# Rotary embedding of the latent attention: a permutation matmul replaced by VectorE products written across partitions

## The reference, cut to what matters

```python
def _rope(x, base):                      # x: (B, S, ..., 64)
    x1, x2 = x[..., :half], x[..., half:]            # half = 32
    return concatenate([x1 * cos - x2 * sin, x2 * cos + x1 * sin], axis=-1)

k_rope = _rope(c[..., KV_LORA:], ROPE_BASE_B)        # once
q_rope = _rope(q[..., QK_NOPE:], ROPE_BASE_B)        # for each head
sc = (einsum('bqhd,bkhd->bhqk', qn_i, k_nope)
      + einsum('bqhr,bkr->bhqk', qr_i, k_rope)) * scale
```

## Time and profile before

| | us |
|---|---|
| median of 3 runs | 906.93 |
| lowest and highest | 906.9, 907.16 |
| the profiled execution's own time | 907.63 |
| its span, first to last instruction | 906.3 |
| TensorE busy | 894.1 (99%) |
| VectorE busy | 592.0 (65%) |
| ScalarE busy | 496.4 (55%) |
| GpSimd busy | 78.2 (9%) |

### The profile page before, as it was taken

One profiled execution on the slowest core, in us unless ns is written; L12 is line 12 of the kernel. 1 busy time (PEld: TensorE's weight loads), 2 busy tenths in 40 slices (PEclk: granted clock), 3 DMA queues, 4 the chain that ended last, 5 costly groups with the idle time before them and its releaser, 6 DMA issues.

```text
span 906.3 us, 13424 instructions
## 1 busy us (share of the span) xinstructions
PE 894.1 (99%) x5649; PEld 798.4 (88%) x5649; DVE 592.0 (65%) x793; ACT 496.4 (55%) x629; POOL 78.2 (9%) x58
## 2 busy tenths in 40 slices
PE   8999999999999999999999999999999999999998
PEld 7798887888899999998887899999899888888887
DVE  5876566559866666666478788766657665566441
ACT  5554444435756666665327677877654355445330
POOL 0010100000001111111000000222200012211000
PEclk9999999999999999999999999999999999999999
DMA  9834554642554444354465544232345535545630
GB/s 348 317 131 182 186 208 166 206 151 99 204 193 141 144 142 142 142 185 182 165 245 174 198 147 180 97 138 93 105 175 187 192 136 184 180 152 212 252 110 24
DMA packets 24829, 154.39 MB, mean 170 GB/s; under 512 B 3136, under 2 KB 3520, under 8 KB 9024
## 3 DMA queue, kind: packets, MB, share of 16 engines
q1 hardware_dynamic: 22880, 148.97, 45.2%
q10 hardware_dynamic: 1728, 4.02, 1.5%
q0 software_dynamic: 160, 0.52, 0.1%
HBM read 152.46 MB, written 1.05 MB: 169 GB/s over the span
## 4 chain that ended last, share of the span: by engine, by line
PE 88%; ACT 5%; DVE 4%; issue 2%; DMA 1%; SPq 0%; ACTq 0%
PE ps L338 23%; PE ps L340 23%; PE ps L339 23%; PE ps L389 7%; PE ps L392 3%; ACT w_hi_ring L966 1%; ACT c_p L1368 1%; PE ps L612 1%; DMA w_raw<-in_a_w_in 1%; PE ps L637 1%; PE ps L617 1%; PE ps L411 1%; PE ps L518 1%; PE ps L806 1%; PE ps L627 1%
## 5 line engine op out<-in xcount | busy, mean ns | idle before, releaser
L1409 DVE TENSOR_TENSOR w_lo_ring<-w_raw,w_hi_ring 128x2048 fp32r<-128x2048 f32 x146 | 341.3, 2351 | 202.2 <-ACT w_hi_ring L966 201.9
L966 ACT ACTIVATE w_hi_ring<-w_raw 128x2048 fp32r<-128x2048 f32 x146 | 277.4, 1910 | 110.9 <-PE ps L340 104.8
L338 PE MATMUL ps<-xT_hi,w_hi_ring 128*128 128x256 f32 x520 | 149.4, 287 | 2.9 <-DVE w_lo_ring L1415 1.7
L340 PE MATMUL ps<-xT_hi,w_lo_ring 128*128 128x256 f32 x520 | 147.0, 283 | 0.0
L339 PE MATMUL ps<-xT_lo,w_hi_ring 128*128 128x256 f32 x520 | 147.0, 283 | 0.0
L338 PE MATMUL ps<-w_hi_ring,xT_hi 128*128 128x512 f32 (+1 forms) x272 | 107.4, 395 | 1.4 <-DVE xT_lo L1586 0.6
L340 PE MATMUL ps<-w_hi_ring,xT_lo 128*128 128x512 f32 (+1 forms) x272 | 104.5, 384 | 0.0
L338 PEld LDWEIGHTS ps<-xT_hi,w_hi_ring 128*128 128x128 f32 x520 | 99.6, 192 | 5.5 <-issue 3.3
L339 PE MATMUL ps<-w_lo_ring,xT_hi 128*128 128x512 f32 (+1 forms) x272 | 104.3, 383 | 0.0
L339 PEld LDWEIGHTS ps<-xT_lo,w_hi_ring 128*128 128x128 f32 x520 | 99.6, 192 | 0.6
L340 PEld LDWEIGHTS ps<-xT_hi,w_lo_ring 128*128 128x128 f32 x520 | 99.6, 192 | 0.0
(11 more groups left out here) (325 smaller groups left out, 1652.2 us busy)
## 6 DMA issues: line engine op xcount, KB each, us to landing
w_raw<-in_a_w_in SPq DMA_DIRECT2D x22, 1024.0 KB, 4.9
w_raw<-in_w_ff_in SPq DMA_DIRECT2D x16, 1024.0 KB, 4.8
w_raw<-in_w_ff_out SPq DMA_DIRECT2D x16, 1024.0 KB, 5.0
w_raw<-in_b_w_uq SPq DMA_DIRECT2D x16, 576.0 KB, 4.4
w_raw<-in_a_w_out SPq DMA_DIRECT2D x8, 1024.0 KB, 4.8
w_raw<-in_b_w_gate SPq DMA_DIRECT2D x8, 1024.0 KB, 4.9
w_raw<-in_kv_w_up SPq DMA_DIRECT2D x8, 1024.0 KB, 4.9
w_raw<-in_b_w_out SPq DMA_DIRECT2D x8, 1024.0 KB, 4.8
```

The source lines that it names most:

```text
L338: k.T.matmul(out, lh, rh, start=start, stop=False, skip_group_check=True)
L340: return k.T.matmul(out, ll, rh, start=False, stop=stop, skip_group_check=True)
L966: k.A.activation(k.hi[:, u % RING, :], k.raw[u % RING][:, :], ACT.Copy).then_inc(k.s["w_hi"], 1)
L1409: k.V.tensor_tensor(k.lo[:, u % RING, :], k.raw[u % RING][:, :], k.hi[:, u % RING, :].bitcast(F32), ALU.subtract).then_inc(k.s["w_lo"], 1)
```

## The change

The permutation matrix, its load, its nine matmuls and the copies to `b_xr` go. VectorE now makes both products straight from PSUM in a function of its own: one on all 128 partitions with the cosines, and four of 32 partitions each with the sines, each of which reads one block of 32 partitions and writes to its neighbour. The table of sines carries the sign. GpSimd keeps only the sum. In the pairs all five products stand where the copy to `b_xr` stood; the product with the sines at L1706 is gone. For the keys they stand where L1645 and L1647 stood.

```diff
@@ place_latent
-    k.b_rope, k.b_rot, k.b_mask = (k.place(n, s) for n, s in (("ropeB", [P, 2, S]), ("rotB", [P, P]), ("maskB", [P, 3 * P])))
+    k.b_rope, k.b_mask = (k.place(n, s) for n, s in (("ropeB", [P, 2, S]), ("maskB", [P, 3 * P])))
@@ pe_pair
     if pair == 0:
-        T.wait_ge(s["b_xr"], 1)
-        T.matmul(ps[:, 7, 0:S], k.b_rot[:, :], k.b_xr[:, :], start=True, stop=True).then_inc(s["b_rotated"], 1)
         T.wait_ge(s["b_lat"], 1)
...
             if q == 2 and n == 0 and pair:
-                T.wait_ge(s["b_sin"], pair)
+                T.wait_ge(s["b_turned"], pair)
...
     m.then_inc(s["w_used"], 1)
-    T.wait_ge(s["b_xr"], pair + 2)
-    T.matmul(ps[:, 2, S:2 * S], k.b_rot[:, :], k.b_xr[:, :], start=True, stop=True).then_inc(s["b_rotated"], 1)
@@ act_program, table loads
-    for name, dst in (("k_ropeB", k.b_rope), ("k_rotB", k.b_rot), ("k_maskB", k.b_mask), ("b_q_norm", k.b_qnorm), ("kv_norm", k.b_kvnorm)):
+    for name, dst in (("k_ropeB", k.b_rope), ("k_maskB", k.b_mask), ("b_q_norm", k.b_qnorm), ("kv_norm", k.b_kvnorm)):
@@ dve_latents
     m.then_inc(s["b_lat"], 1)
-    V.tensor_copy(k.b_xr[:, :], ps[:, 6, 0:S]).then_inc(s["b_xr"], 1)
+def dve_rotary(k, x):
+    k.V.tensor_tensor(k.b_xc[:, :], x, k.b_rope[:, 0, :], ALU.mult)
+    for n in range(4):
+        src, dst = slice(32 * n, 32 * n + 32), slice(32 * (n ^ 1), 32 * (n ^ 1) + 32)
+        m = k.V.tensor_tensor(k.b_xs[dst, :], x[src, :], k.b_rope[src, 1, :], ALU.mult)
+    return m
@@ dve_key_rotary
-    V.wait_ge(s["b_xr"], 1)
-    own.mark(V.tensor_tensor(k.b_xc[:, :], k.b_xr[:, :], k.b_rope[:, 0, :], ALU.mult))
-    V.wait_ge(s["b_rotated"], 1)
-    own.mark(V.tensor_tensor(k.b_xs[:, :], ps[:, 7, 0:S], k.b_rope[:, 1, :], ALU.mult))
+    own.mark(dve_rotary(k, k.ps[:, 6, 0:S]))
     own.wait()
@@ dve_pair
     if pair:
-        V.wait_ge(s["b_cos"], pair)
-    V.tensor_copy(k.b_xr[:, :], ps[:, 2, 0:S]).then_inc(s["b_xr"], 1)
+        V.wait_ge(s["b_qr"], pair)
+    else:
+        V.wait_ge(s["b_kr"], 1)
+    dve_rotary(k, ps[:, 2, 0:S]).then_inc(s["b_turned"], 1)
...
-    V.wait_ge(s["b_rotated"], pair + 2)
-    if pair:
-        V.wait_ge(s["b_qr"], pair)
-    V.tensor_tensor(k.b_xs[:, :], ps[:, 2, S:2 * S], k.b_rope[:, 1, :], ALU.mult).then_inc(s["b_sin"], 1)
@@ pool_program
-        G.wait_ge(s["b_xr"], pair + 2)
...
-        G.tensor_tensor(k.b_xc[:, :], k.b_xr[:, :], k.b_rope[:, 0, :], ALU.mult).then_inc(s["b_cos"], 1)
-        G.wait_ge(s["b_cos"], pair + 1)
-        G.wait_ge(s["b_sin"], pair + 1)
+        G.wait_ge(s["b_turned"], pair + 1)
         G.tensor_tensor(k.b_qr[:, pair % 2, :], k.b_xc[:, :], k.b_xs[:, :], ALU.add).then_inc(s["b_qr"], 1)
```

More of the change, by code:

```diff
@@ L71 @@
     "o_prod", "ln_t0", "ln_t1",
-    "b_squared", "b_qlat", "b_lat", "b_xr", "b_rotated", "b_kr", "b_gate", "b_scored", "b_pmax", "b_masked", "b_pexp", "b_p",
-    "b_pturned", "b_pT", "b_valued", "b_og", "b_oT_hi", "b_oT_lo", "b_qn", "b_cos", "b_sin", "b_qr", "b_kn", "b_v",
+    "b_squared", "b_qlat", "b_lat", "b_kr", "b_gate", "b_scored", "b_pmax", "b_masked", "b_pexp", "b_p",
+    "b_pturned", "b_pT", "b_valued", "b_og", "b_oT_hi", "b_oT_lo", "b_qn", "b_turned", "b_qr", "b_kn", "b_v",
     "c_sq", "c_total", "c_h0", "c_h1", "c_drain_a", "c_drain_v", "c_kw_hi", "c_kw_lo", "c_sp_in", "c_sp_exp", "sc_even",
@@ L203, in place_latent @@
     k.b_qr, k.b_p, k.b_pT = (k.place(n, [P, 2, c]) for n, c in (("b_qr", S), ("b_p", 3 * P), ("b_pT", 3 * P)))
-    k.b_xr, k.b_xc, k.b_xs = (k.place(n, [P, S]) for n in ("b_xr", "b_xc", "b_xs"))
+    k.b_xc, k.b_xs = (k.place(n, [P, S]) for n in ("b_xc", "b_xs"))
     k.b_og = k.place("b_og", [P, 2, S])
@@ L703, in keys_read @@
     def keys_read():
-        T.wait_ge(s["b_sin"], last + 1)
+        T.wait_ge(s["b_turned"], last + 1)
         T.wait_ge(s["b_kn"], last + 1)
@@ L1100, in act_latents @@
         if n == 0:
-            A.wait_ge(s["tablesB_in"], 16 * 5)
+            A.wait_ge(s["tablesB_in"], 16 * 4)
         act_turned(k, "qlat", n, ps[:, 1 + n, :], k.b_qlatT[0], k.b_qnorm)
@@ L1617, in dve_latents @@
     V, s, ps, own = k.V, k.s, k.ps, k.v_own
-    V.wait_ge(s["tablesB_in"], 16 * 5)
+    V.wait_ge(s["tablesB_in"], 16 * 4)
     for n in range(4):
@@ L1637, in dve_latents @@
     m.then_inc(s["b_lat"], 1)
-    V.tensor_copy(k.b_xr[:, :], ps[:, 6, 0:S]).then_inc(s["b_xr"], 1)
-def dve_key_rotary(k):
-    V, s, ps, own = k.V, k.s, k.ps, k.v_own
-    V.wait_ge(s["b_xr"], 1)
-    own.mark(V.tensor_tensor(k.b_xc[:, :], k.b_xr[:, :], k.b_rope[:, 0, :], ALU.mult))
-    V.wait_ge(s["b_rotated"], 1)
-    own.mark(V.tensor_tensor(k.b_xs[:, :], ps[:, 7, 0:S], k.b_rope[:, 1, :], ALU.mult))
+def dve_rotary(k, x):
[4 more added lines that the diff above has]
+    return m
+def dve_key_rotary(k):
+    own = k.v_own
+    own.mark(dve_rotary(k, k.ps[:, 6, 0:S]))
     own.wait()
-    V.tensor_tensor(k.b_kr, k.b_xc[:, :], k.b_xs[:, :], ALU.add).then_inc(s["b_kr"], 1)
+    k.V.tensor_tensor(k.b_kr, k.b_xc[:, :], k.b_xs[:, :], ALU.add).then_inc(k.s["b_kr"], 1)
 def dve_softmax(k, pair, h):
@@ L2040, in pool_program @@
         G.tensor_tensor(k.a_o[:, 0, :], k.a_o[:, 0, :], k.a_g[:, 0, :], ALU.mult).then_inc(s["a_gated0"], 1)
-    G.wait_ge(s["tablesB_in"], 16 * 5)
     for pair in range(HB // 2):
@@ L2166, in constants @@
     ang = np.tile(rope_angles(ROPE), (2 * P // ROPE, 1))
[L2167 to L2175, removed]
+    sign = np.where(np.arange(P)[:, None] % ROPE < ROPE // 2, 1.0, -1.0)
+    out["k_ropeB"] = np.stack([np.cos(ang), sign * np.sin(ang)], 1).astype(f)
     causal = np.where(np.arange(P)[None, :] <= np.arange(P)[:, None], 0.0, -1.0e30).astype(f)
```

## The result

| | before | changed |
|---|---|---|
| median of 9 runs, us | 907.16 | 909.59 |
| lowest and highest | 906.86, 907.34 | 909.06, 910.15 |
| span of the profiled execution | 906.3 | 908.2 |

The ratio is 1.0029 (95% interval 1.0020 to 1.0038): 2.4 us slower. The forecast was 909.0, in a range of 905.3 to 910.6.

The account below looks back on a forecast made before the run. TensorE, busy 99% of the span, was taken to bound the kernel. 907.63 - 1.24 (pair 0) + 3.2 (7 x 0.46, pairs 1 to 7) = 909.6; on the runs' median 908.9, rounded to 909.0; range 905.3 to 910.6.

Parts of the forecast that it names:

- Pair 0 gains 1.24 us.: TensorE in pair 0: 0.43 us from L686 and 0.81 us from L651 leave its queue, together 1.24 us gained.
- the 0.81 of L651: Pair 0 on TensorE: without L651 the latent's transposes wait for `b_lat` alone and start at 246.94, not 247.75.
- The cover of `b_latT_lo`: Keys' part, pair 0: `b_latT_lo` starts 1.04 us later and ends near 253.1; TensorE needs it at 254.2, cover 1.1 us.
- The products do not overlap.: VectorE, five products ahead of the second head's softmax: priced at 0.43 us each, 2.15 us in all, instead of 0.34 each.
- The memset behind them gets 0.03.: VectorE, behind the five products: 0.03 us for the memset, making the block 2.18 us and the softmax 1.84 us later.
- The delay runs over ScalarE into `b_pT`, with 1.38 us to spare.: Pairs 1 to 7: later softmax delays ScalarE's rounded copy, then `b_pT`; beyond 1.38 us TensorE loses 0.46 us a pair.
- TensorE idle 0.9 us ahead of the second head's L637.: Sign in pairs 1 to 7: TensorE waits about 0.9 us before the second head's values, put down to ScalarE.
- A pair every 23.3 us.: Sign for the pitch of the pairs: 23.3 us instead of 22.83 between VectorE's copies.
- The covers.: Later `b_og`, `b_v`, `b_qr` and the dropped table load cost nothing; `b_og` and `b_v` have over 3 us.

Follow-up runs that it names:

- e8: Changed kernel with six small products a pair instead of four, the last two into spare tiles; 915.05 us, ratio 1.0097 to the kernel before.
- e3: Kernel before with only the keys' rotary part in pair 0 changed, the queries' part kept; 906.38 us, ratio 0.9993.
- e1: Changed kernel with all four sine products of a pair reading and writing partitions 0 to 31, into spare tiles; 905.22 us, ratio 0.9981 to before.
- e6: Changed kernel with the pairs' four sine products reading blocks 0, 32, 64, 96, all writing partitions 0 to 31 of spare tiles; 908.17 us, ratio 1.0020.
- e7: Changed kernel with the pairs' four sine products all reading partitions 0 to 31, writing to 0, 32, 64, 96 in turn; 908.14 us, ratio 1.0018.
- e2: Changed kernel with the five products of a pair behind the second head's softmax, not ahead of it; 903.17 us, ratio 0.9957 to before.
- e4: Changed kernel with two small products a pair instead of four, the second head's sine part left out; 903.47 us, ratio 0.9960 to before.

## Why the prediction was right

- *Pair 0 gains 1.24 us.* Measured 1.36, 1.35 in e8 and 1.23 to 1.25 in the other experiments with both changes; e3 gives the 0.81 of L651 by itself as 0.8. The cover of `b_latT_lo` held: TensorE shows no wait for it.
- *The products do not overlap.* Right, and e1 shows it is the change of partitions. Each start costs 0.42 to 0.44, taken as 0.43. The rule of the Trainium skill, "VectorE: DVE Perf Modes", section "Two Vector instructions with no wait between them", agrees in each of e1, e6, e7 and the changed kernel: a start is held back to the end of all before it when the block read or the block written is another than last time. The Trainium skill's other page, "Vector Engine (DVE) Microarchitecture Reference", section 3.8, which calls such moves free, holds here for an instruction's length (0.41 to 0.43 us on 32 partitions across, 0.42 on 128 in place) and not for its start.
- *The memset behind them gets 0.03.* This was the term that was sized too small. The last product is followed by 0.06 us of issue, 0.06 of memset and 0.01, so the block is 2.28 and not 2.18, and the delay 1.94, not 1.84.
- *The delay runs over ScalarE into `b_pT`, with 1.38 us to spare.* Right in mechanism, by e2, e4 and e8; the spare time is 1.40 in this kernel. The seven pairs lose 3.8 us where 3.2 were forecast: 0.54 each instead of 0.46, the longer block (+0.10) less the larger reserve (-0.02). Less the 0.12 that pair 0 gains beyond its forecast, that is the difference between the forecast's +2.0 and the trace's +2.4. Measured 909.59 against the forecast 909.0 holds 0.2 us more, since before itself came out at 907.16 and not 906.93.
- *TensorE idle 0.9 us ahead of the second head's L637.* The sum is about right, the place is not: the text had `b_p` ready after TensorE would turn it (282.25 against 281.74), but counted no wait there. In the trace the larger wait is at L627, recorded as 0.51 us idle, and a smaller one of 0.19 follows at L637. From start to start TensorE loses 0.67 ahead of L627 (280.73, where 279.94 + 0.12 was due) and 0.32 from there to the second head's L637 (1.39 against 1.07 before): 0.99 in all, of which 0.44 is the matmul that went.
- *A pair every 23.3 us.* (416.0 - 275.74) / 6 = 23.38, with 416.0 the last start of L1639.
- *The covers.* `b_og`, `b_v`, `b_qr`, the table loads: no wait of TensorE for any of them appears in the waits from 240 to 450 us, and what lies ahead of `b_lat` has not grown (245.09 against 245.42).

That the time came out beyond 0.2% above before was less sure than it looks: e6 and e7, with a block shorter by 0.21 us, lie at +0.18 to 0.20%. The 0.43 a product was a choice that no row of before tested against 0.34, as the prediction says itself; the experiments bear it out.

## What to carry to other kernels

Taking work off the engine that bounds the kernel gains nothing if what takes its place stands ahead of the work that this engine needs next; before counting the gain, follow the displaced instruction over every engine to the point where the bound engine takes it up, and see how much time is to spare on the way (here 1.4 us on ScalarE). The same instructions a few lines further down VectorE's queue turned +2.4 us into -3.7. And a row of short VectorE instructions that hop between blocks of 32 partitions costs its full recorded lengths, not the distances at which neighbours on the same partitions start; count the return as well.

## What the runs showed of the hardware that was not expected

GpSimd's sum `b_qr`, 0.74 us long as a rule (median of 8), took 2.84 us in pair 0 of the changed kernel. It started 0.05 us behind a remainder of VectorE and ended 0.60 us behind it:

```profile
259.42 2.29 DVE L1405 TENSOR_TENSOR w_lo_ring<-w_raw,w_hi_ring 128x2048 fp32r<-128x2048 f32 x1
259.47 2.84 POOL L2045 TENSOR_TENSOR b_qr<-b_xc,b_xs 128x256 f32<-128x256 f32 x1 [96.06 <-DVE b_xs L1642]
```

In e1 it started 0.15 us behind the remainder, took 2.72 us and again ended 0.60 us behind it. In pair 1 of the kernel before it was the other way round: `b_qr` ran first, and the remainder that started 0.15 us behind it was recorded with 2.74 us instead of 2.29:

```profile
287.88 2.74 DVE L1409 TENSOR_TENSOR w_lo_ring<-w_raw,w_hi_ring 128x2048 fp32r<-128x2048 f32 x1 [2.05 <-ACT w_hi_ring L966]
```

In pair 0 of the kernel before, `b_qr` (261.96, 0.74 us) ran beside VectorE's copy of `b_v` from PSUM (261.74, 0.68 us), and both kept their lengths. The two engines appear to take turns on operations whose inputs all lie in SBUF, the one that comes second waiting for the first. Here it cost nothing, since the scores came 4.4 us later (266.7 against 262.3); a chain that relies on a short GpSimd operation should count the longest VectorE operation it can fall behind. No run tested this by itself.
